# Order of the high and low products on TensorE, and the addresses of their operands modulo 512 bytes

## The reference

```
for i in range(DEPTH):                       # first block
    z = rmsnorm(x, g_mix[i]) @ w_in[i]       # 2048 -> 4928
    ... mla attention, short conv, gated conv, retention ...
    x = x + concat([y_a, y_b, y_c, y_d]) @ w_o[i]
    uf = causal_dwconv(rmsnorm(x, g_ffn[i]) @ w_up[i], w_ffn_conv[i])
    gate, up = split(uf, 2)
    x = x + (silu(gate) * up) @ w_down[i]    # 5632 -> 2048
    x = x + (p[i] @ w_pe[i]) * sigmoid(rmsnorm(x, g_pe[i]) @ w_pg[i])
for l in range(DEPTH):                       # second block
    p = rms_norm(x, norm_g[l]) @ w_in[l]
    ... fox, diff and moba attention, gated linear attention ...
    x = x + mixed @ w_out[l]
return rms_norm(x, final_norm_g)
```

## Time and profile before

| | |
|---|---|
| median of 3 runs | 3373.32 us |
| profiled execution | 3373.81 us |
| its span on the core | 3371.7 us |
| TensorE products (PE) | 3336.6 us busy, 99% of the span, 20334 instructions |
| TensorE weight loads (PEld) | 2895.6 us, 86% |
| VectorE (DVE) | 2610.3 us, 77% |
| ScalarE (ACT) | 1529.8 us, 45% |
| GpSimd (POOL) | 863.3 us, 26% |
| mean DMA rate | 179 GB/s |

### The profile page before, as it was taken

The page is one execution under the profiler, slowest core; times in us unless marked ns, Lnnn a source line. Parts: engine busy times, 40 slices in busy tenths (PEclk is TensorE's granted clock), DMA queues, the critical chain, the costliest instruction groups (busy, mean ns, idle before and its releaser), DMA issues. The chain is left out here.

```text
span 3371.7 us, 53679 instructions
## 1 busy us (share of the span) xinstructions
PE 3336.6 (99%) x20334; PEld 2895.6 (86%) x20334; DVE 2610.3 (77%) x3392; ACT 1529.8 (45%) x1642; POOL 863.3 (26%) x633
## 2 busy tenths in 40 slices
PE   8999999999999999999999999999999999999998
PEld 7988888888888889888888888888878888888887
DVE  7887788787786878877887787867867866677775
ACT  5654444343433556544443434335444444444443
POOL 0432333121122423414331121214432004150004
PEclk9999999999999999999999999999999999999999
DMA  6445555555555554445555555556544455544454
GB/s 230 157 152 181 190 189 187 176 201 177 205 174 189 200 179 165 148 170 190 192 187 177 198 179 201 176 188 202 188 163 150 163 175 189 180 163 150 163 186 151
DMA packets 90648, 605.21 MB, mean 179 GB/s; under 512 B 10192, under 2 KB 10353, under 8 KB 29297
## 3 DMA queue, kind: packets, MB, share of 16 engines
q1 hardware_dynamic: 89424, 599.83, 51.9%
q10 hardware_dynamic: 1056, 3.11, 0.3%
HBM read 600.80 MB, written 2.10 MB: 179 GB/s over the span
## 5 line engine op out<-in xcount | busy, mean ns | idle before, releaser
L639 PE MATMUL bank<-H,whi 128*128 128x512 f32 x6496 | 1606.2, 397 | 15.9 <-DVE H L1677 13.7
L1155 ACT ACTIVATE whi<-raw 128x2048 fp32r<-128x2048 f32 (+2 forms) x609 | 1093.6, 1796 | 1092.4 <-DMA raw<-in_slabs_down 263.0
L1621 DVE TENSOR_TENSOR wlo<-raw,whi 128x2048 fp32r<-128x2048 f32 (+2 forms) x609 | 1325.8, 2177 | 248.2 <-ACT whi L1155 240.6
L639 PEld LDWEIGHTS bank<-H,whi 128*128 128x128 f32 x6496 | 1186.9, 188 | 278.4 <-issue 21.3
L648 PEld LDWEIGHTS bank<-H,wlo 128*128 128x128 f32 x6624 | 833.1, 188 | 39.7
L648 PE MATMUL bank<-H,wlo 128*128 128x256 f32 x6624 | 852.3, 277 | 0.0
L511 POOL TENSOR_TENSOR sqtmp<-tmp 128x256 f32<-128x256 f32 x88 | 219.1, 2490 | 869.6 <-DVE tmp L2201 869.6
L639 PE MATMUL bank<-G,whi 128*128 128x512 f32 x1408 | 348.7, 394 | 0.0
L639 PEld LDWEIGHTS bank<-G,whi 128*128 128x128 f32 x1408 | 254.8, 188 | 52.2
L1555 ACT ACTIVATE G<-sqtmp 128x256 f32 (+1 forms) x88 | 36.8, 418 | 402.9 <-POOL sqtmp L511 402.9
L1642 DVE TENSOR_REDUCE tmp<-bank 128x256 f32<-128x512 f32 x216 | 149.0, 690 | 76.8 <-PE bank L648 76.0
(11 more groups left out here) (387 smaller groups left out, 2856.5 us busy)
## 6 DMA issues: line engine op xcount, KB each, us to landing
raw<-in_slabs_up SPq DMA_DIRECT2D x176, 1024.0 KB, 4.9
raw<-in_slabs_down SPq DMA_DIRECT2D x128, 704.0 KB, 4.0
raw<-in_slabs_wo SPq DMA_DIRECT2D x32, 1024.0 KB, 4.9
raw<-in_slabs_pg SPq DMA_DIRECT2D x32, 1024.0 KB, 4.9
raw<-in_slabs_gates SPq DMA_DIRECT2D x32, 1024.0 KB, 4.9
raw<-in_slabs_wout SPq DMA_DIRECT2D x32, 1024.0 KB, 4.9
raw<-in_slabs_sc SPq DMA_DIRECT2D x24, 1024.0 KB, 4.9
raw<-in_slabs_fox SPq DMA_DIRECT2D x24, 1024.0 KB, 4.9
```

The source lines that it names most:

```text
L639: pe.matmul(b[0:r.m, :], whi[:, n % RAW, w], r.src[:, k, :], start=at == 0, stop=False)
L1155: act.activation(whi[:, n % RAW, 0:w], raw[:, n % RAW, 0:w], ACT.Copy).then_inc(S("hi_ready"), 1)
L1621: dve.tensor_tensor(wlo[:, n % RAW, 0:w], raw[:, n % RAW, 0:w], whi[:, n % RAW, 0:w].bitcast(F32), ALU.subtract).then_inc(S("lo_ready"), 1)
```

## The change

In `run` the inner loops become one: for each tile k the high product is issued and directly behind it the low one, in all slabs. `step` is gone. The attention's small products go behind 8 of 16 pairs, the side work (`advance`) behind 12 of 16 pairs, and `h_free` is signalled after pairs 4, 8 and 12 as before.

The pads around `H` go, and pads come around `whi`. Modulo 512 bytes `H`, `G`, `cq` and `z` now start at 128, `wlo` at 128, `whi` at 448, and `pT_hl` stays at 320. So, of the products of `run` on `H` and `G`, low weights are 0 off (192 before) and high weights 192 off (as before). In `value_slab` the streams are the weights: 128 - 320 = 320 off before, for both; 448 - 128 = 320 off now for `whi`, and 0 off for `wlo`.

```
-    sb("ahead_of_H", [P, 48])
     H = sb("H", [P, DC, 2 * T], F32R)
-    sb("behind_H", [P, 80])
...
     wlo = sb("wlo", [P, RAW, 2048], F32R)
+    sb("ahead_of_whi", [P, 80])
     whi = sb("whi", [P, RAW, 2048], F32R)
+    sb("behind_whi", [P, 48])
...
-    sb("ahead_of_z", [P, 24])
+    sb("ahead_of_z", [P, 104])
...
-                step = 1 if opening or not streams_both(key) else 4 if handed else r.kt
-                for first in range(0, r.kt, step):
-                    chunks = range(first, min(first + step, r.kt))
-                    for at in chunks:
...
-                        if base is not None and at == (r.kt * 3 // 4 if step == r.kt else r.kt // 2):
-                            (within_first if key[0] in STAGES else within_slab)(key[1], base + 4 * i + j)
...
-                            pe.matmul(b[0:r.m, :], whi[:, n % RAW, w], r.src[:, k, :], start=at == 0, stop=False)
...
-                    for at in chunks:
...
-                        if at == (r.kt // 4 if step == r.kt else r.kt * 6 // 8):
-                            advance(beside, 1)
-                        last = pe.matmul(b[0:r.m, 0:T], wlo[:, n % RAW, w], r.src[:, k, 0:T], start=False,
-                                         stop=at == r.kt - 1)
...
+                for at in range(r.kt):
+                    k = at if order is None else order[at]
...
+                    if at == r.kt * 6 // 8:
+                        advance(beside, 1)
+                    if base is not None and at == r.kt // 2:
+                        (within_first if key[0] in STAGES else within_slab)(key[1], base + 4 * i + j)
...
+                    if streams_both(key):
+                        pe.matmul(b[0:r.m, :], whi[:, n % RAW, w], r.src[:, k, :], start=at == 0, stop=False)
...
+                    last = pe.matmul(b[0:r.m, 0:T], wlo[:, n % RAW, w], r.src[:, k, 0:T], start=False,
+                                     stop=at == r.kt - 1)
```

More of the change, by code:

```diff
@@ L622, in run @@
                 b = bank_of(r, n)
-                handed = key[0] in HANDED and isinstance(i, int) and 4 * i + j == r.count - 1
-                step = 1 if opening or not streams_both(key) else 4 if handed else r.kt
-                for first in range(0, r.kt, step):
-                    chunks = range(first, min(first + step, r.kt))
-                    for at in chunks:
[L628 to L632, removed]
-                        if base is not None and at == (r.kt * 3 // 4 if step == r.kt else r.kt // 2):
-                            (within_first if key[0] in STAGES else within_slab)(key[1], base + 4 * i + j)
[L635 to L638, removed]
-                            pe.matmul(b[0:r.m, :], whi[:, n % RAW, w], r.src[:, k, :], start=at == 0, stop=False)
-                        else:
-                            pe.matmul(b[0:r.m, 0:T], whi[:, n % RAW, w], r.src[:, k, 0:T], start=at == 0, stop=False)
-                            pe.matmul(b[0:r.m, 0:T], whi[:, n % RAW, w], r.src[:, k, T:2 * T], start=False, stop=False)
-                    for at in chunks:
-                        k = at if order is None else order[at]
-                        w = slice(k * r.m, (k + 1) * r.m)
-                        if at == (r.kt // 4 if step == r.kt else r.kt * 6 // 8):
-                            advance(beside, 1)
-                        last = pe.matmul(b[0:r.m, 0:T], wlo[:, n % RAW, w], r.src[:, k, 0:T], start=False,
-                                         stop=at == r.kt - 1)
-                        if handed and at in (3, 7, 11):
-                            last.then_inc(S("h_free"), 1)
@@ new lines, in run @@
+                for at in range(r.kt):
+                    k = at if order is None else order[at]
+                    if opening and at == 0:
+                        pe.wait_ge(S("h_ready"), 12)
+                    if opening and at % 4 == 0:
+                        pe.wait_ge(*((S("lo_ready"), 1) if at == 12 else (S("lo_part"), at // 4 + 1)))
+                    if at == r.kt * 6 // 8:
+                        advance(beside, 1)
+                    if base is not None and at == r.kt // 2:
+                        (within_first if key[0] in STAGES else within_slab)(key[1], base + 4 * i + j)
+                    if operand is not None and j == 0 and (i == 0 if isinstance(i, int) else r.loop):
+                        operand(k)
+                    w = slice(k * r.m, (k + 1) * r.m)
+                    if streams_both(key):
+                        pe.matmul(b[0:r.m, :], whi[:, n % RAW, w], r.src[:, k, :], start=at == 0, stop=False)
+                    else:
+                        pe.matmul(b[0:r.m, 0:T], whi[:, n % RAW, w], r.src[:, k, 0:T], start=at == 0, stop=False)
+                        pe.matmul(b[0:r.m, 0:T], whi[:, n % RAW, w], r.src[:, k, T:2 * T], start=False, stop=False)
+                    last = pe.matmul(b[0:r.m, 0:T], wlo[:, n % RAW, w], r.src[:, k, 0:T], start=False,
+                                     stop=at == r.kt - 1)
+                    if key[0] in HANDED and isinstance(i, int) and 4 * i + j == r.count - 1 and at in (3, 7, 11):
+                        last.then_inc(S("h_free"), 1)
```

## The result

The changed kernel takes 3391.93 us (median of 4 runs, 3390.03 to 3395.04), the kernel before beside it 3372.95 (4 runs, 3372.41 to 3373.91). The ratio is 1.0057, with a 95% interval of 1.0044 to 1.0069: 19.0 us slower. The forecast was 3405, between 3300 and 3430. The direction holds, and so does that the order costs and the pads take a part of it back. Three terms of the sum don't hold, and what lies beneath them is the more useful thing to learn from this case.

The account below looks back on a forecast made before the run. The prediction took TensorE, full at full clock, as the bound: time is the sum of product costs. The profiled 3373.8 us + 31.6 for the order, pads and rest at 0, less 0.5, gave 3405 us, range 3300 to 3430.

Parts of the forecast that it names:

- The bound: Whole kernel: TensorE has a product under way in 99% of the span, at full clock; nothing else to remove.
- The order term: Pairs on `H` and `G`: taking turns costs 4.4 and 2.2 ns a pair more, +31.6 us.
- +47.4: Same pairs on `H` and `G`, priced by the opening slab's last three pairs, 353.3 ns: +47.4 us.
- The pads, taken at 0: Low weights going from 192 to 0 off: nothing taken, -13 to +7 ns a pair kept as range.
- the pads gain: Rival, pairs in turns: load at 0 off never meets the stream again; 340 ns a pair, 3316 us; chance 0.31.
- Its sign: High products in turns under 229 ns would decide for the case that the pads do more.
- The rest, taken at 0: Products of 256 columns in turns (+8 or -11 us possible), value slabs and small products: no change taken.
- 1.3 was the bound: Value slabs: a third of 960 products goes from 320 to 0 off, 1.3 us either way.
- In loops and outside alike: Any `up` slab after: pairs of 351 to 353 ns, low product near 118, high near 235.
- The pads undo the price of turns: Rival, pairs in turns: the 0-off load takes one step back; 346.7 ns a pair, 3369 us; chance 0.13.
- 325 ns a pair: The skill page's estimate for a pair in either order, said to give 3203 us; no-stall rival's chance 0.02.
- No wait moves: Slabs: small products, side work and signals keep nearly their times; VectorE, busy 83%, only gains room.

Follow-up runs that it names:

- e2_turns_old_pads: The changed kernel's turns with the pads of the kernel before (both weights 192 off): 3418.51 us, ratio 1.0138.
- e3_steer264: The changed kernel plus 9 products of 264 columns, each ahead of the third slab of a `high_first` run, output overwritten: 3345.29 us, ratio 0.9914.
- e1_groups_new_pads: The groups of the kernel before (16 high, then 16 low) with the changed kernel's pads: 3414.85 us, ratio 1.0120.
- m2_starts: Bench of float32r products alone, not the reference's work: five cases of order and offsets, 17 starts each; no total time given.
- e5_steer_more: e3_steer264 with 264 columns added ahead of the second `pg` slab too, and 272 instead of 264 in `wo` of layer 0: 3343.75 us.
- e7_steer268: e5_steer_more with 268 columns in the added products of `pg` and of `wo` of layer 0: 3343.68 us, ratio 0.9912.
- e4_groups_high0_low192: The groups of the kernel before, with high weights 0 off and low weights 192 off: 3370.28 us, ratio 0.9991.
- m1_offsets: Bench of float32r products alone: 64 combinations of the two weights' offsets, turns from three starts, then groups of 12; no total time given.

## Why the prediction was right, and where its steps were not

**The bound.** Right. TensorE is at 99% before and after, with a mean granted clock of 0.998 in both, and the whole difference lies in the distances between its products.

**The number.** The forecast of 3405 came within 13 us of 3392 partly by luck: the order cost about 12 us more than its term and the pads gave back 27 against a term of nothing.

**The order term, +31.6 us.** Mis-sized. Alone the order costs 44 us (e2_turns_old_pads), near the +47.4 that I had worked out beside it and not taken. The step that failed is taking the mean of the eight opening pairs, 351.3 ns, for the price, as an allowance for the pads: it holds the first pairs at full clock, and first pairs are cheaper (about 346 ns in e2_turns_old_pads) until the stretch has settled. The last three pairs, 353.3, were the price of all its settled stretches. The reason given for the price, that the load's read meets the stream's, isn't shown. The runs show that the price hangs on order, addresses and start with all other engines idle, and not where in TensorE's path it arises.

**The pads, taken at 0 with -13 to +7 ns a pair.** Wrong in size. Given turns they bring 26.6 us (3418.5 to 3391.9); the pairs alone gain 29.7, on the average 3.8 ns a pair, inside the bounds. Given groups they cost 40 us. The remark that they might take back part of the order's price was right, and lowering the order's term for it made the total look better than its terms. The chance of 0.31 for "the pads gain" went to a case that 6 of the 25 stretches of after are in, and that e3_steer264 puts 19 of its 25 in: 340.0 ns was worked out rightly as a price, and what I hadn't seen is that the same code may run at either. Its sign, a high product under 229 ns, holds too: 226.8 ns in the stretches at 340, 232.1 in those at 350.

**The rest, taken at 0.** It is +5 us. `high_first` and the other products of 256 columns cost +3.9, inside the +8 that I gave as its end. But they don't answer to the pads alone, as I had it: in e2_turns_old_pads, with the pads of before, they cost the same 3.9 more, though their own order is unchanged. The value slabs cost +2.8, where 1.3 was the bound. They answer to the pads alone: 228.8 us in after and in e1_groups_new_pads, 226.0 before and 225.8 in e2_turns_old_pads. A product there went from 229.6 to 233.2 ns on average, and the ones that stream `wlo` from 229.3 to 234.5, more than the 4 ns that I had allowed. Those on `whi` got dearer too (229.7 to 232.5), though their offset is as it was. The +1.3 us counted the changed third alone, and that was the fault; why the others follow isn't shown.

**In loops and outside alike, one price of 351 to 353.** Wrong. Stretches differ, 340.0 or 350.0, and none of over 40 pairs settles at 351 or more. The low product near 118 is right in the stretches at 350 (117.9), the high one near 235 isn't (232.1).

**The pads undo the price of turns.** The rival's price, 346.7 ns, exists, but at other addresses: m2_starts has it from all 17 starts with the high weights at 0 off and the low ones at 192, not the other way round as in after.

**Slips.** 325 ns a pair would give some 3198 us, not 3203, and the chances of the single cases add up to 0.34 for faster and 0.12 for same, not 0.35 and 0.11. Neither moves the forecast. And not all tiles between the weights and `z` are multiples of 512 bytes, as the description of the kernel has it (`eps` is one number wide); the remainders given there hold.

**No wait moves.** Right; the idle time is 13.8 us against 15.9. VectorE's 340.77 us of 412 in the same window as the earlier trace rows had the room that was expected:

```profile
400.00:812.00 412.00, 412.00 (x2356) 362.36 (x2355) 340.77 (x428) 166.73 (x144) 106.57 (x64) 1.00 0.54 186
```

**What stays open.** Which part of the chip makes the grid of 6.67 ns, and by what rule a start picks the price; with it one could set all stretches to 340, and e5_steer_more and e7_steer268 show that I don't have it. The stretch at 77 us shows that a price can change between executions of the same instructions, and what decides it there isn't known. It needn't be what spreads the runs. Those of after spread by 5.0 us and the 15 of before beside e4_groups_high0_low192 by 5.4, and the mean granted clock may have a part in it: the longest run of after, 3395.04 us, has 0.997, the two shortest 0.998. A product ahead of the groups of e4_groups_high0_low192 wasn't tried.

## What to carry to other kernels

When TensorE is full, compare kernels by the distance between starts, stretch by stretch, and take the settled price, never a mean that includes the first pairs. Don't judge an order with one placement of the buffers only, nor a placement with one order: here each edit alone cost 40 us or more and both together 19. And before a slower time is laid at a change's door, look whether one stretch of the same code runs at two prices; if so, a small shift of where the stretch begins may be worth more than the change (here 47 us for 9 added products). Settle such a question by many runs or by a control that differs in the start alone, since a single stretch may change its price by itself.

## What the runs showed of the hardware that was not expected

- Products of float32r behind each other don't cost their columns at full clock (213 + 107 = 320 ns a pair at 2.4 GHz). In the kernels' long stretches of turns and in m2_starts a settled pair of 512 and 256 columns took 340.0, 346.7, 350.0 or 353.3 ns, of this 227 to 235 for the 512 columns: the pair's 51, 52, 52.5 and 53 steps of 6.67 ns. Some combinations in m1_offsets settle into patterns of two or three pairs with other means, 349 to 352 ns. At the lower clock level the same pair took 640 ns, its columns and no more.
- The price hangs on both weight tiles' addresses modulo 256 bytes, on the order, and on the moment the stretch begins: m1_offsets and m2_starts show all three with all other engines idle.
- Once settled, a price held for up to some 2,000 pairs (from 394.3 us to the end of `down`, 1101.2, in e3_steer264, at 340.0 throughout), across banks, slabs and other transfers.
- Eight more streaming columns in 9 of 20343 products took the kernel from 3393.6 to 3345.3 us.
- The same 64 pairs, with nothing changed ahead of them, settled at 340.0 ns in after and at 350.0 in e3_steer264.
